# One step of a hybrid encoder layer on one core: the eighth dot directly behind the seventh, attention's queries and keys on a semaphore of their own with the key copies last, and the first values of semaphores set by four engines

## What is computed

```python
h = rmsnorm(x, norm1_g) * (1 + scale1) + shift1
z, xbc, dt_raw, q, k, v, gates = split(h @ w_in)
y_ssm = ssd_branch(z, xbc, dt_raw, ...)            # Mamba-2, 32 heads
o = banded_attention(q, k, v, sinks)               # prompt; samples: cached_attention
x = x + gate1 * ((g_ssm * (y_ssm @ w_branch_ssm) + g_attn * (o @ w_branch_attn)) @ w_out)
h2 = rmsnorm(x, norm2_g) * (1 + scale2) + shift2
x = x + gate2 * peer_ffn(h2, ...)                  # 16384 experts, 8 heads x 16 picks a token
# peer_ffn: act = gelu(u[eidx] . t);  out = sum over picks of (w * act) * v[eidx]
```

## Time and profile before

| | |
|---|---|
| median of 3 runs | 5161.06 us (5156.77 to 5169.4) |
| the profiled execution's own time | 5159.56 us |
| its span in the profile | 5157.8 us |
| PE busy | 4588.6 us (89%) |
| DVE busy | 3583.0 us (69%) |
| ACT busy, POOL busy | 1806.4 us (35%), 1519.4 us (29%) |
| attention, from barrier to barrier | 1672.5 to 1927 us |
| experts, from barrier to barrier | 3123.2 to 5090 us |

### The profile page before, as it was taken

How to read it: one execution, slowest core, us unless ns; L and a number is a source line. 1 busy time by engine, 2 the same in 40 slices (tenths; PEclk the granted TensorE clock), 3 DMA queues, 4 the chain that set the end, 5 groups by cost and what they waited for, 6 DMA issues and landing times. The chain is left out here.

```text
span 5157.8 us, 83514 instructions
## 1 busy us (share of the span) xinstructions
PE 4588.6 (89%) x28775; PEld 4250.4 (82%) x28775; DVE 3583.0 (69%) x6876; ACT 1806.4 (35%) x3735; POOL 1519.4 (29%) x1356
## 2 busy tenths in 40 slices
PE   5999999688887889996988578999999999999995
PEld 3999999587777559996887467999999999999994
DVE  3110555455554552344999997999999999999996
ACT  3111333232322553222444693333333333333331
POOL 0000000011110000000000004777777777777772
PEclk8999999888888779997999899999999999999997
DMA  3232222223232324433999358999999999999995
GB/s 155 101 134 94 82 95 91 111 92 113 98 107 75 65 60 153 176 140 122 349 337 342 147 195 320 362 361 368 369 371 365 371 357 366 367 364 372 372 363 195
DMA packets 350799, 1170.33 MB, mean 227 GB/s; under 512 B 40129, under 2 KB 91457, under 8 KB 344257
## 3 DMA queue, kind: packets, MB, share of 16 engines
q0 software_dynamic: 147456, 536.94, 27.8%
q1 hardware_dynamic: 160480, 483.07, 26.2%
q10 hardware_dynamic: 42720, 148.52, 7.6%
HBM read 971.20 MB, written 197.46 MB: 227 GB/s over the span
## 5 line engine op out<-in xcount | busy, mean ns | idle before, releaser
L2167 POOL DMA_INDIRECT ex_ur<-scr_u_rows,ex_at x512 | 613.2, 1198 | 303.9 <-DVE ex_ur L2342 123.4
L2169 POOL DMA_INDIRECT ex_vr<-in_expert_v,ex_at x512 | 631.3, 1233 | 223.2 <-issue 152.0
L2350 DVE SCALAR_TENSOR_TENSOR ex_acc_rows<-ex_vr,ex_wt,ex_acc_rows 128x1024 f32<-128x1024 f32 x512 | 651.4, 1283 | 40.8 <-ACT ex_wt L2272 37.3
L2342 DVE SCALAR_TENSOR_TENSOR ex_ur<-ex_ur,h_rows 128x1024 f32<-128x1024 f32 x512 | 620.9, 1222 | 10.2 <-DMA ex_ur<-scr_u_rows,ex_at 9.8
L915 POOL TENSOR_TENSOR sd_cts<-sd_cT,sd_ea 128x512 f32<-128x512 f32 x72 | 92.2, 1281 | 1521.8 <-ACT sd_ea L873 1521.8
L2161 POOL COPY ex_at<-picked_at 128x4 uint32 x128 | 67.9, 530 | 1509.7 <-POOLq L121 1509.2
L2179 PE MATMUL ex_ps<-hd_hi,ex_u_hi 128*128 128x320 f32 x2048 | 470.3, 311 | 20.6 <-PEq L121 18.6
L2179 PE MATMUL ex_ps<-hd_hi,ex_u_lo 128*128 128x320 f32 x2048 | 468.6, 310 | 0.0
L2179 PE MATMUL ex_ps<-hd_lo,ex_u_hi 128*128 128x320 f32 x2048 | 468.6, 310 | 0.0
L2270 ACT ACTIVATE ex_gel<-ex_dot 128x1 f32<-128x1 f32 x512 | 103.9, 203 | 987.9 <-DVE ex_ur L2342 987.9
L457 DVE TENSOR_TENSOR pr_w_lo<-pr_w,pr_w_hi 128x1024 fp32r<-128x1024 f32 x58 | 71.1, 1226 | 512.5 <-ACT pr_w_hi L453 512.5
(11 more groups left out here) (350 smaller groups left out, 11422.3 us busy)
## 6 DMA issues: line engine op xcount, KB each, us to landing
pk_raw_u<-in_expert_u SPq DMA_DIRECT2D x128, 512.0 KB, 6.2
scr_u_rows<-pk_rows_u ACTq DMA_DIRECT2D x128, 512.0 KB, 6.2
ex_u<-in_expert_u SPq DMA_DIRECT2D x128, 512.0 KB, 7.1
ex_v<-in_expert_v SPq DMA_DIRECT2D x128, 512.0 KB, 8.5
scr_gate<-gt_stage SPq DMA_DIRECT2D x10, 4096.0 KB, 12.6
ex_gate<-scr_gate SPq DMA_DIRECT2D x32, 1280.0 KB, 8.9
pr_w<-in_w_main SPq DMA_DIRECT2D x58, 512.0 KB, 4.6
scr_xbc<-pr_out ACTq DMA_DIRECT2D x32, 576.0 KB, 3.7
```

What stands on the lines that cost most here:

```text
L2167: nc.gpsimd.indirect_dma_start(out=ur[:, s], out_offset=None, in_=scr["u_rows"], in_offset=by).then_inc(ur_in[s], 16)
L2169: nc.gpsimd.indirect_dma_start(out=vr[:, s], out_offset=None, in_=io["expert_v"].rearrange("j i d -> (j i) d"), in_offset=by).then_inc(vr_ ...
L2342: v.scalar_tensor_tensor(out=ur[:, s], in0=ur[:, s], scalar=1.0, in1=rows[:, s], op0=ALU.mult, op1=ALU.mult, accum_out=dot[:, m:m + 1]).th ...
L2350: v.scalar_tensor_tensor(out=acc_g[:, s], in0=vr[:, s], scalar=wt[:, m:m + 1], in1=acc_g[:, s], op0=ALU.mult, op1=ALU.add).then_inc(row_r[ ...
```

## The change

It has three parts.

1. In `open_`, the first value of a semaphore is added by one of four engines, by its hardware number modulo 4: GpSimd, VectorE, ScalarE or SyncE.
2. In attention, queries and keys have a semaphore of their own (`qk_in`), the other four tiles another (`kv_in`). PE's first scores and ACT's copy wait for the first; PE waits for the second ahead of the first `values` and of the scores of the last tile. The two key copies are issued after all loads.
3. In experts, DVE's `dots(b, 7)` stands directly behind `dots(b, 6)`, and `add_rows(b, 7)` ahead of `add_sums(b, 7)`.

```diff
@@ open_
         for s in got:
             if at:
-                nc.gpsimd.sem_inc(s, at)
+                starter = (nc.gpsimd, nc.vector, nc.scalar, nc.sync)[s.num % 4]
+                starter.sem_inc(s, at)
@@ phase_attention
-        small, loaded, qs_r = sem("at_small"), sem("at_in", 2), sem("at_qsr", 2)
+        small, qk_in, kv_in, qs_r = sem("at_small"), sem("at_qk_in", 2), sem("at_kv_in", 2), sem("at_qsr", 2)
@@ SP
-            for n, t in (("k_prompt", NT - 2), ("k_sample", LAST)):
-                sp.dma_start(io[n][:], scr["plain"][TK:TK + MK, :, t * P:(t + 1) * P]).then_inc(copied, 16)
             with sp.Fori(0, NKV // 2) as i:
...
-                    sp.dma_start(qT[:, s], heads(scr["plain"], TQ + g * 2, 2)).then_inc(loaded[s], 16)
+                    sp.dma_start(qT[:, s], heads(scr["plain"], TQ + g * 2, 2)).then_inc(qk_in[s], 16)
...
+            for n, t in (("k_prompt", NT - 2), ("k_sample", LAST)):
+                sp.dma_start(io[n][:], scr["plain"][TK:TK + MK, :, t * P:(t + 1) * P]).then_inc(copied, 16)
@@ PE, scores and values
                 if c == 0:
-                    pe.wait_ge(loaded[s], i * 96 + 96 + START)
+                    pe.wait_ge(qk_in[s], i * 32 + 32 + START)
...
                     pe.wait_ge(qs_r[s], i + 1 + START)
+                    pe.wait_ge(kv_in[s], i * 64 + 64 + START)
...
                 pe.wait_ge(oc_r[q], u + START)
+                if c == 0:
+                    pe.wait_ge(kv_in[s], i * 64 + 64 + START)
@@ ACT
-                    act.wait_ge(loaded[s], i * 96 + 96 + START)
+                    act.wait_ge(qk_in[s], i * 32 + 32 + START)
@@ phase_experts, DVE, batch
                     dots(b, 6)
+                    dots(b, 7)
                     add_rows(b, 6)
                     add_sums(b, 6)
-                    dots(b, 7)
                     if more:
                         rest_of_u(b + 2, 1)
+                    add_rows(b, 7)
                     add_sums(b, 7)
-                    add_rows(b, 7)
```

More of the change, by code:

```diff
@@ L1109, in _ @@
                     sp.wait_ge(o_st[s], i * 16 + START)
-                    sp.dma_start(qT[:, s], heads(scr["plain"], TQ + g * 2, 2)).then_inc(loaded[s], 16)
-                    sp.dma_start(kT[:, s], scr["plain"][ds(TK + i, 1)][:, s * DH:(s + 1) * DH].rearrange("m d t -> d (m t)")).then_inc(loaded[s], 16)
-                    sp.dma_start(v[:, s], scr["vd"][:, :, ds(g * DH, DH)]).then_inc(loaded[s], 16)
-                    sp.dma_start(vn[:, s], scr["vd"][:, LAST, ds(g * DH, DH)].rearrange("(b t) d -> t b d", t=TS)).then_inc(loaded[s], 16)
-                    sp.dma_start(kc[:, s], io["k_cache"][ds(g, 1)].rearrange("g d b k -> d (g b) k")).then_inc(loaded[s], 16)
-                    sp.dma_start(vc[:, s], io["v_cache"][ds(g, 1)].rearrange("g k b d -> k (g b) d")).then_inc(loaded[s], 16)
+                    sp.dma_start(qT[:, s], heads(scr["plain"], TQ + g * 2, 2)).then_inc(qk_in[s], 16)
+                    sp.dma_start(kT[:, s], scr["plain"][ds(TK + i, 1)][:, s * DH:(s + 1) * DH].rearrange("m d t -> d (m t)")).then_inc(qk_in[s], 16)
+                    sp.dma_start(v[:, s], scr["vd"][:, :, ds(g * DH, DH)]).then_inc(kv_in[s], 16)
+                    sp.dma_start(vn[:, s], scr["vd"][:, LAST, ds(g * DH, DH)].rearrange("(b t) d -> t b d", t=TS)).then_inc(kv_in[s], 16)
+                    sp.dma_start(kc[:, s], io["k_cache"][ds(g, 1)].rearrange("g d b k -> d (g b) k")).then_inc(kv_in[s], 16)
+                    sp.dma_start(vc[:, s], io["v_cache"][ds(g, 1)].rearrange("g k b d -> k (g b) d")).then_inc(kv_in[s], 16)
+            for n, t in (("k_prompt", NT - 2), ("k_sample", LAST)):
+                sp.dma_start(io[n][:], scr["plain"][TK:TK + MK, :, t * P:(t + 1) * P]).then_inc(copied, 16)
             sp.wait_ge(copied, 32 + START)
```

## The result

| | before | after |
|---|---|---|
| median | 5165.2 us (4 runs, 5156.8 to 5172.2) | 5085.7 us (4 runs, 5076.7 to 5095.0) |
| ratio, 95% interval | | 0.9847 [0.9822, 0.9872] |
| the profiled execution's own time | 5159.6 us | 5095.0 us |

The profiled execution of the changed kernel is the slowest of its four, so that the two profiles differ by 64.6 us only.

A forecast was written before the change was run, and what follows sets the result against it. Phases follow behind full barriers; in experts DVE sets a plain batch's length, with PE and gathers close behind. From 5159.6, 19.0 (first values), 5.5 (attention) and 14 (dot) leave 5121 us, 5122 beside the median; range 5103 to 5141.

The forecast's parts named there:

- The assumed 80 ns for all engines: First values: each addition costs 80 ns on any engine, so 25.9 us become 6.9 and 19.0 are saved.
- first values don't run side by side: Rival (0.08): other engines pay far more or the barrier takes the saving; part 1 worth 5 or less, time 5136.
- The wait for the values: Attention, PE's new wait ahead of the first `values`: more than 10 us of cover, so none of the 5.5 lost.
- The gather for `dots(b, 3)`: Experts, fourth dot of a gate batch: its gather does not move earlier, so the batch gives its 0.6 us back.
- The signs named for it: Profile of experts: no DVE wait for `ex_wt`, but over 13 u-gather waits, 0.6 to 1.0 us at gate batches' fourth dot.
- the eighth dot: Experts, `dots(b, 7)` needs its gather 2.2 us earlier: cover 1.5 plain, 0.3 gate; 0.1 to 0.2 us new gate wait.
- The plain batch at 29.5: Experts: plain batches take 29.5 us between equal dots, DVE's batch being 0.60 us shorter.
- PE's piece and the sum ahead of it: Experts: `add_sums(b, 6)` ends at 4022.6, just in time for PE's eighth piece, which started at 4022.59.
- the term of 14: Part 3 in experts: about 0.45 us per plain and gate pair, 32 pairs, 14 us saved; ends 0 and 38.
- Experts are bound by DMA: Rival (0.22): DVE's new idle time goes to gather waits; part 3 worth -5 to 5 us, time 5136.
- Everything is given: Rival (0.11): gathers land earlier as DVE frees slots earlier; part 3 worth 28 to 38 us, time 5098 to 5108.
- Slower: Rival (0.04): the gather of `dots(b, 7)` lands late; slower above 0.98 us of new wait in every batch.

The follow-up runs named there:

- Part 1 alone: Only the spreading of first values over four engines, against the kernel before: 5122.6 against 5156.5 us, ratio 0.9930.
- e6_tail_swap: Kernel before with only `add_rows(b, 7)` moved ahead of `add_sums(b, 7)`, the eighth dot in its old place: 5160.7 us, ratio 1.0003.
- e5_fill: Kernel before with a fill of zeros in place of each batch's fifth dot; run once, read from its profile: experts 1979.6 us.

## Why the prediction was wrong

Of the 40 us by which the forecast was short, 20 are part 3's and 15 part 1's; the rest is within the interval. Without the 15 of part 1 the time would have been near the range's lower end of 5103.

**Part 1: the mechanism right, the sum too small.** The forecast was 19.0, and the stretches gave 18.6. The assumed 80 ns for all engines is near: from start to start it is 78 ns on GpSimd, 59 on SyncE, 72 on ScalarE and 93 on VectorE. The sum took it for granted that the phases behind stay as long as they were, and this failed. Part 1 alone took 34 us off, some 10 of the other 15 in the state space phase; why stays open. The rival "first values don't run side by side" is refuted.

**Part 2: right.** Forecast 5.5, measured 4.9 at the start of the scores. The keys landed 1.1 earlier and not 1.7, since `at_kT` was issued 2.59 us behind the barrier (3.53 before) and took 9.1 to land (9.3). The wait for the values cost nothing that shows: the scores' wait is PE's only one for a load in the phase.

**Part 3: the failed step.** "The gather for `dots(b, 3)`": "POOL's order of issues hangs on the batch before (its first free is `add_rows(b, 0)`, then some 20 us of POOL's own work), not on DVE's last dots. When DVE arrives 0.6 earlier, the gather does not. So a gate batch gives its 0.6 back at this place." GpSimd's own work is no fixed time: its 16 gathers of a batch took 19.4 us (1244.5 us over 64 batches, both groups of the page), where 16 undisturbed ones are 15.0; the other 4.4 are holding by DVE's instructions, and the reordered DVE holds 1.4 us less in just this stretch. The gather arrives earlier with DVE, and the gate batch keeps its 0.6 and also loses the wait that it had, so that it gains 0.98 where nothing was forecast. The row that would have told me was in sight: the gathers in the earlier trace rows last 1.96, 1.20 and 0.94 us, and I took their lengths as given.

The sum of this part has a slip besides: 0.6 + 0.6 - 0.6 - 0.15 is 0.45 a pair, and less the 0.05 to 0.2 it is 0.25 to 0.4, which gives 8 to 13 us and not 14. The signs named for it did not come: more than 13 waits for u gathers, of 0.6 to 1.0 us at the fourth dot of gate batches, were expected, and there are 10 in single batches.

The forecast for the eighth dot was right in kind: the cover is 1.2 us in a plain batch and 0.4 in a gate batch (1.5 and 0.3 forecast), and DVE waits there only in single batches. The plain batch at 29.5 was right (29.45). PE's piece and the sum ahead of it were right (PE's waits fell to 7.4 us). Against the batch's gain of 52 us, part 3 is worth 34: some 18 are lost in single batches whose gathers come late, about half of them behind gathers of 4.93 us. So the term of 14 should have been 52 less this.

**The rivals.** "Experts are bound by DMA" is refuted: a gate batch now moves 411 GB/s at a DMA share of 1.02 and does not wait. The Trainium skill's 358 GB/s for the HBM side (DMA: Bandwidth & Descriptors, section Bandwidth) was no bound here; its 435 for the ports stays above all rows. "Everything is given" (0.11) was right for part 3, and its 5098 to 5108 too high by part 1's extra. "Slower" did not come near: no wait for a gather in normal batches.

## What to carry to other kernels

Before a gather's time is taken as a constant, see whether its duration varies with the same data, and at what DVE does at its start: an order of DVE's instructions that puts sums from PSUM, or an instruction's end, where a gather begins, takes tenths of a microsecond off GpSimd's time. That pays only where a gather is late (e6_tail_swap: nothing), and the whole phase has to be looked at, not one batch: the same order let a few gathers be held for 4.93 us. A wait for several tiles on one semaphore costs what lies between the first and the last that is needed (here 3.9 us). And price a short edit by its own place, but measure it alone as well: the phases behind may move by as much as the edit, with TensorE's clock, and one profile of one kernel can't tell this apart.

## What I had not expected of the hardware

- A gather takes 0.94 us, or until 0.81 us behind the end of a DVE instruction that reads two operands from SBUF (698 of 699 held gathers of the kernel before). Seldom one is passed over and held to the end of a later one: five instructions and 4.93 us in the changed kernel (5 gathers), 2.98 us with a fill between in e5_fill.
- One semaphore addition every 59 ns on SyncE, 72 on ScalarE, 78 on GpSimd, 93 on VectorE and 151 on TensorE, though the durations shown are 17 to 51 ns.
- A phase that no edit touched takes 724 to 744 us in eighteen kernels, with 182 to 215 us of it at the lower level of TensorE's clock.
